# A hybrid attention block on one core: order of the front part, index units held back, narrower waits

## The reference

```python
h = rms_norm(x, g_in[layer])
proj = h @ w_in[layer]
...
mem_n = rms_norm(mem, g_mem[layer])
kvM = mem_n @ w_mem_kv[layer]
...
logits = jnp.einsum('bqhc,bsc->bqhs', qib, kI).astype(jnp.float32) * (IDX_DIM ** -0.5)
score = jnp.einsum('bqh,bqhs->bqs', wib.astype(jnp.float32) * (N_IDX_HEADS ** -0.5),
                   jax.nn.relu(logits))
```

## Time and profile before

| | us |
|---|---|
| runs: median of 3 (lowest, highest) | 741.73 (740.82, 744.18) |
| the profiled execution | 743.63 |
| its span, first to last instruction | 741.8 |
| PE busy in it | 677.5 |
| DVE busy | 421.9 |
| ACT busy | 334.4 |
| POOL busy | 145.3 |
| mean granted TensorE clock | 0.990 |

### The profile page before, as it was taken

How to read it: one execution, slowest core, us unless ns; L and a number is a source line. 1 busy time by engine, 2 the same in 40 slices (tenths; PEclk the granted TensorE clock), 3 DMA queues, 4 the chain that set the end, 5 groups by cost and what they waited for, 6 DMA issues and landing times.

```text
span 741.8 us, 11508 instructions
## 1 busy us (share of the span) xinstructions
PE 677.5 (91%) x4261; PEld 539.1 (73%) x4261; DVE 421.9 (57%) x985; ACT 334.4 (45%) x629; POOL 145.3 (20%) x96
## 2 busy tenths in 40 slices
PE   2999999999999999999999899879999997999992
PEld 2777788777778777877777677657878776777771
DVE  3946765276397676677478748972343354122245
ACT  5776564325335343534353336442564584111224
POOL 2021110111222111401231141104111166112002
PEclk9999999999999999999999999999999999999997
DMA  8421102111211121112111311101110424510004
GB/s 284 132 74 38 30 29 58 29 29 43 86 43 29 45 86 44 29 43 86 43 30 44 86 42 30 43 2 43 43 29 20 166 79 172 169 43 22 1 29 198
DMA packets 51863, 47.71 MB, mean 64 GB/s; under 512 B 5712, under 2 KB 44640, under 8 KB 51808
## 3 DMA queue, kind: packets, MB, share of 16 engines
q1 hardware_dynamic: 51808, 46.97, 20.4%
HBM read 39.62 MB, written 7.34 MB: 63 GB/s over the span
## 4 chain that ended last, share of the span: by engine, by line
PE 72%; DVE 13%; issue 5%; ACT 4%; DMA 2%; POOL 2%; SPq 1%; DVEq 0%; ACTq 0%; POOLq 0%
PE j_ps L1415 22%; PE s_ps L1415 9%; PE o_ps L1546 7%; PE pt_ps L1522 6%; PE s_ps L1451 5%; PE s_ps L1596 4%; PE j_ps L1596 4%; PE o_ps L1415 4%; PE s_ps L1470 3%; DVE picked L1172 2%; PE pt_ps L1470 2%; DVE probT L1256 2%; DVE prob L1247 1%; PE s_ps L1601 1%; PE pt_ps L1568 1%
## 5 line engine op out<-in xcount | busy, mean ns | idle before, releaser
L1415 PE MATMUL j_ps<-h_hi,w_hl 128*128 128x512 f32 (+2 forms) x640 | 208.8, 392 | 1.7 <-issue 0.9
L1415 PEld LDWEIGHTS j_ps<-h_hi,w_hl 128*128 128x128 f32 (+1 forms) x640 | 118.8, 187 | 26.3 <-issue 2.7
L690 POOL TENSOR_TENSOR w_hl<-w_raw,w_hl 128x1024 fp32r<-128x1024 f32 (+1 forms) x29 | 68.2, 2352 | 333.3 <-ACT w_hl L792 320.8
L1415 PE MATMUL j_ps<-h_lo,w_hl 128*128 128x512 f32 (+2 forms) x320 | 122.5, 383 | 0.0
L966 ACT ACTIVATE prob<-prob,nmax 128x256 f32<-128x256 f32 (+7 forms) x128 | 89.9, 704 | 57.9 <-DVE nmax L1247 52.2
L954 ACT ACTIVATE probT<-pt_ps 128x512 f32<-128x512 f32 (+3 forms) x88 | 41.2, 468 | 136.8 <-PE pt_ps L1522 136.2
L1522 PE MATMUL pt_ps<-ident,prob 128*128 128x128 f32 x496 | 74.0, 281 | 11.0 <-DVE probT L1256 4.0
L1522 PEld LDWEIGHTS pt_ps<-ident,prob 128*128 128x128 f32 x496 | 54.9, 141 | 28.9 <-issue 22.3
L1415 PE MATMUL s_ps<-h_hi,w_hl 128*128 128x512 f32 x224 | 74.2, 399 | 0.0
L1172 DVE TENSOR_SCALAR_CACHE_REDUCE picked<-idx,tk 128x384 f32<-128x384 f32 (+5 forms) x72 | 67.8, 942 | 1.2
L1415 PEld LDWEIGHTS j_ps<-h_lo,w_hl 128*128 128x128 f32 (+1 forms) x320 | 59.9, 187 | 10.9
(11 more groups left out here) (239 smaller groups left out, 1104.5 us busy)
## 6 DMA issues: line engine op xcount, KB each, us to landing
w_raw<-in_w_in_dram SPq DMA_DIRECT2D x27, 512.0 KB, 3.9
idx<-in_x_dram SPq DMA_DIRECT2D x8, 512.0 KB, 6.6
bias<-in_a_tab_dram SPq DMA_DIRECT2D x8, 512.0 KB, 4.4
mixed_scratch<-gate SPq DMA_DIRECT2D x12, 256.0 KB, 2.2
bias<-in_x_dram SPq DMA_DIRECT2D x4, 512.0 KB, 8.9
probT<-in_w_mem_kv_dram SPq DMA_DIRECT2D x4, 512.0 KB, 6.4
bias<-in_w_out_dram SPq DMA_DIRECT2D x4, 512.0 KB, 3.7
out_dram<-idx SPq DMA_DIRECT2D x4, 512.0 KB, 4.2
```

Of the source, the lines that this page charges most:

```text
L690: pool.tensor_tensor(w_hl[:, w % 2, 1, :, 0:n], raw_of(w)[:, :, 0:n], w_hl[:, w % 2, 0, :, 0:n].bitcast(F32), ALU.subtract).then_inc(w_lo_ ...
L1415: last = pe.matmul(bank[0:n, at:], a[:, k, 0:n], c[:, k, HALF * b + at:HALF * b + HALF], start=(k == 0 and q == 0), stop=(k == KD - 1 and ...
```

## The change

1. `idx_schedule` keeps the last two units of pairs 0, 1 and 2 back (`HELD_UNITS`) and puts them behind the last step of the projection that they are woven into.
2. The row that ACT scales has a semaphore of its own, `x_scaled`; `x_ready` counts DVE's rows alone. POOL's first weight split waits for three DVE rows, no longer for four of both.
3. The first 24 transposes go row by row, in the order 0, 3, 1, 2, each row waiting for itself alone; a bank is announced at its piece of row 2.
4. Ahead of them PE makes 26 transposes of the identity into `j_ps` (`stay_busy`), in three groups: after ACT's first square sum, after its second, and after the first variance.
5. ACT's square sums of rows 4 and 6 stand behind the eight high parts of the first half, DVE's of row 5 behind its eight low parts.
6. Unit 2, no longer unit 0, waits for w_i's evacuation.
7. q0's first half comes before `memturn`; `memturn` waits for the memory projections only. `scores(0)` no longer waits for the front's last evacuation, the first `values` does.

```diff
@@ -230,6 +230,7 @@
 PAIRS_I = H_I // 2
 IDX_UNITS = [(i, 2 * j + a) for j in range(PAIRS_I) for a in range(2) for i in IDX_TILES]
 PER_PAIR = 2 * len(IDX_TILES)
+HELD_UNITS = 2
 X_OFF = {i: sum(P * (q + 1) for q in range(FIRST_TOPK, i)) for i in IDX_TILES}
 X_COLS = sum(P * (q + 1) for q in IDX_TILES)
 
@@ -272,14 +273,14 @@
     for j in range(PAIRS_I):
         if j + 1 < PAIRS_I:
             mine = [m for m, (kind, w, _) in enumerate(uses) if kind == "w" and w == W_OF["qI", j + 1]]
-            head, each = 4, 1
+            head, each, kept = 4, 1, HELD_UNITS
         else:
             mine = [m for m, (kind, _, _) in enumerate(uses) if kind == "mem"]
-            head, each = 8, 2
+            head, each, kept = 8, 2, 0
         units = list(range(PER_PAIR * j, PER_PAIR * (j + 1)))
         for n, (m, k) in enumerate([(m, k) for m in mine for k in range(KD)]):
             out.append(("fill", m, k))
-            if n >= head - 1 and (n - head + 1) % each == each - 1 and units:
+            if n >= head - 1 and (n - head + 1) % each == each - 1 and len(units) > kept:
                 out.append(("unit", units.pop(0), None))
         out += [("unit", u, None) for u in units]
     return out
@@ -388,6 +389,7 @@
         var_ready = sem("var_ready")
         root_ready = sem("root_ready")
         x_ready = sem("x_ready")
+        x_scaled = sem("x_scaled")
         turned = sem("turned")
         hi_ready = sem("hi_ready")
         lo_ready = sem("lo_ready")
@@ -474,8 +476,8 @@
 
         uses = [("w", w, b) for b in range(2) for w in range(2)] + [("wturn", 0, 0)]
         uses += [("w", W_OF["qI", j], b) for j in range(1, PAIRS_I) for b in range(2)]
-        uses += [("mem", w, 0) for w in range(4)] + [("memturn", 0, 0)]
-        uses += [("w", W_OF["q", 0], b) for b in range(2)]
+        uses += [("mem", w, 0) for w in range(4)]
+        uses += [("w", W_OF["q", 0], 0), ("memturn", 0, 0), ("w", W_OF["q", 0], 1)]
         n_pre = len(uses)
         steps_of_uses = [s for s in range(STEPS) if projection_of_step(s)]
         uses += [("w", *projection_of_step(s)) for s in steps_of_uses]
@@ -716,7 +718,7 @@
                 pool.tensor_tensor(qk[:, PART_SLOT[p] + 1, tokens], gates(p)[:, tokens],
                                    qk[:, PART_SLOT[p], tokens].bitcast(F32), ALU.subtract).then_inc(part_lo_ready, 1)
 
-            pool.wait_ge(x_ready, NT // 2)
+            pool.wait_ge(x_ready, NT // 2 - 1)
             for w in range(PRE_W + 1):
                 split_lo(w)
             mask_diagonal(0)
@@ -864,7 +866,7 @@
             act.activation(stat[:, 2, 0:1], rungs[:, 0, 0:1], ACT.Sqrt).then_inc(root_ready, 1)
             def scale_row(r, chain):
                 act.wait_ge(x_inverse, chain)
-                act.activation(x_raw[r], x_raw[r], ACT.Copy, scale=stat[:, 3, r:r + 1]).then_inc(x_ready, 1)
+                act.activation(x_raw[r], x_raw[r], ACT.Copy, scale=stat[:, 3, r:r + 1]).then_inc(x_scaled, 1)
 
             square_sum(0)
             square_sum(2)
@@ -873,11 +875,11 @@
             split_hi(0)
             scale_row(3, 1)
             split_hi(1)
-            square_sum(4)
-            square_sum(6)
             act.wait_ge(g_ready, 1)
             for v in range(KD):
                 high(v)
+            square_sum(4)
+            square_sum(6)
             root(4, 8)
             evacuate(0)
             scale_row(7, 2)
@@ -906,7 +908,7 @@
                     evacuate(n)
                     if uses[n][0] == "w" and uses[n][2] == 1:
                         split_hi(uses[n][1] + 2)
-            m = use_number["memturn", 0, 0]
+            m = use_number["w", W_OF["q", 0], 0]
             evacuate(m)
             evacuate(m + 1)
             evacuate(m + 2)
@@ -1075,9 +1077,9 @@
             square_sum(1)
             dve.wait_ge(g_ready, 1)
             scale_rows(0, 4, 3)
-            square_sum(5)
             for v in range(KD):
                 low(v)
+            square_sum(5)
             square_sum(7)
             scale_rows(4, 8, 5)
 
@@ -1357,7 +1359,8 @@
             def turn(v):
 
                 half, k = v // KD, v % KD
-                pe.wait_ge(x_ready, NT // 2 * (half + 1))
+                pe.wait_ge(x_ready, (NT // 2 - 1) * (half + 1))
+                pe.wait_ge(x_scaled, half + 1)
                 if v >= 6:
                     pe.wait_ge(lo_ready, v - 5)
                 for c in range(4):
@@ -1368,7 +1371,7 @@
             def turn_mem(n):
 
                 if n == 0:
-                    pe.wait_ge(x_ready, NT + MT)
+                    pe.wait_ge(x_ready, NT - 2 + MT)
                     pe.wait_ge(lo_ready, 2 * KD)
                 for a in range(2):
                     for t in range(MT):
@@ -1391,7 +1394,7 @@
                         last = pe.matmul(bank[:, 0:N_MEM], wm_raw[:, w % 2, k, :], memT[:, k, :],
                                          start=(k == 0), stop=(k == KD - 1))
                 elif kind == "memturn":
-                    pe.wait_ge(j_free, m)
+                    pe.wait_ge(j_free, use_number["mem", 3, 0] + 1)
                     for t in range(MT):
                         for f in range(2):
                             at = N_MEM * t + P * f
@@ -1417,10 +1420,29 @@
                 if kind not in ("w", "mem") or ks[-1] == KD - 1:
                     last.then_inc(j_done, 1)
 
+            def stay_busy(turns):
+
+
+                for n in range(turns):
+                    pe.transpose(j_ps[:, P * (n % 4):P * (n % 4) + P], ident[:, :], ident[:, :])
+
             pe.wait_ge(rows_in, 32)
             pe.transpose(o_ps[:, 0:2 * KD], g_rows[:, :], ident[0:2 * KD, 0:2 * KD]).then_inc(g_turned, 1)
-            for v in range(6):
-                turn(v)
+            pe.wait_ge(squares_ready, 1)
+            stay_busy(8)
+            pe.wait_ge(squares_ready, 2)
+            stay_busy(8)
+            pe.wait_ge(var_ready, 1)
+            stay_busy(10)
+            for n, r in enumerate([0, 3, 1, 2]):
+                if r == 3:
+                    pe.wait_ge(x_scaled, 1)
+                else:
+                    pe.wait_ge(x_ready, r + 1)
+                for v in range(6):
+                    last = pe.transpose(turn_banks[v][:, P * r:P * r + P], x_raw[r][:, P * v:P * v + P], ident[:, :])
+                    if n == 3:
+                        last.then_inc(turned, 1)
             pe.wait_ge(g_ready, 1)
             fill(0, range(0, 2))
             turn(6)
@@ -1460,7 +1482,8 @@
                     if u == 0:
                         pe.wait_ge(k_copied, 2)
                         pe.wait_ge(mem_ready, KD)
-                        wait_evacuated(pe, use_number["wturn", 0, 0])
+                if u == 2:
+                    wait_evacuated(pe, use_number["wturn", 0, 0])
                 if u >= 3:
                     pe.wait_ge(relu_ready, u - 2)
                 tile = slice(P * i, P * i + P)
@@ -1493,7 +1516,6 @@
                     lent = [m for m, b in enumerate(bank_ids) if b == 3 and steps_of_uses[m - n_pre] < s]
                     wait_evacuated(pe, lent[-1])
                 if s == 0:
-                    pe.wait_ge(j_free, n_pre)
                     pe.wait_ge(relu_ready, len(IDX_UNITS))
                 else:
                     for a in range(2):
@@ -1531,6 +1553,8 @@
                     pe.wait_ge(pt_ready[a], g + 1)
                 if i % 4 == 0 and c == 0 and (p, i // 4) in V_TURNS:
                     pe.wait_ge(v_kept, v_turns_before(p, i // 4) + 1)
+                if s == 0:
+                    wait_evacuated(pe, n_pre - 1)
                 if i % 4 == 0 and c == 0 and s >= 4:
                     pe.wait_ge(og_ready, s // 4)
                 at = slice(P * (i % 4), P * (i % 4) + P)
```

## The result

| | before | changed | again (both once more) |
|---|---|---|---|
| median of the runs, us | 743.39 (6 runs) | 734.65 (6 runs) | 743.36 (13) and 734.65 (6) |
| lowest, highest | 740.82, 745.49 | 733.03, 738.12 | |
| ratio to before, 95% interval | | 0.989 [0.9865, 0.9915] | 0.9885 [0.9864, 0.9906] |
| span of the profiled execution | 741.8 | 731.3 | 731.8 |
| mean granted TensorE clock | 0.990 | 0.988 | 0.992 |

The change takes 8.7 us off, 1.1%, where 7.65 were forecast. With more runs of before its median is 743.4, so the profiled execution of before (743.63) was an ordinary one and not 1.9 us over it.

The account below looks back on a forecast made before the run. TensorE was taken as the bound, busy 677.5 of 741.8 us. Savings of 0.8 + 1.25 + 3.8 + 1.7 + 0.1 = 7.65 us from 743.63 gave 736.0 us, range 733.6 to 738.9.

Parts of the forecast that it names:

- Front: Program start to the second half's transposes: row-by-row transposes and later square sums save 0.8 us, bounds -0.2 to 1.8.
- the taking of 15.6 us for the clock's rise: In the first row transposes: TensorE reaches full clock at 15.6, with 8.6 transposes cold and 9.4 warm.
- L: Time of the first low product up front: 20.05 before, forecast 17.75; between 16.7 and 18.8 was the sign.
- The rule against the fillers: Skill's sentence that transposes don't count as clock activity, against the identity transposes up front; forecast held that the trace disagrees.
- First index unit: Unit 0 no longer waits for w_i, only for the memory rows' last copy: 1.25 us saved, bounds 0.9 to 1.25.
- Held units: First units of pairs 1 and 2: two kept-back units cover TensorE's idle, 1.9 us each, 3.8 us in all.
- T: 65.80 before: qI1's last matmul has passed, qI2's first is issued; pair 1's first unit then started 3.39 later.
- Clock: At 87.5 to 92 us, the 1.2 GHz stretch behind TensorE's idle goes: 1.7 us saved, bounds 0 and 1.7.
- q0: End of the index part: q0's first half ahead of the memory turn saves 0.1 us, bounds 0 and 1.0.
- The clock paid again: Rival: a cold stretch follows a new idle before the second half or q0's second half, costing 1.7: 737.7 us, 18%.
- The moved gap: Rival at the first units of pairs: the projection's split stays as late, no gain from held units or clock: 741.5, 10%.
- the backed-up adds: Rival: held adds behind POOL's split delay unit 17, three steps each lose 2.4 plus 1.7: 748.3 us, 4%.

Follow-up runs that it names:

- again: The changed kernel, same code, timed and profiled once more beside the kernel before: 734.65 us, ratio 0.9885.
- nofill: The changed kernel without the 26 transposes of the identity: 734.81 us, ratio 0.9897.
- holdonly: The kernel before with only the two held units added: 736.70 us, ratio 0.9915.
- best_nofill: The changed kernel without identity transposes, row 5's square sum on ScalarE, memory turn in pt_ps, step 0's projection not waiting for the last evacuation and split: 732.30 us.
- hold0: The changed kernel with no held units (HELD_UNITS = 0): 740.40 us, ratio 0.9955.
- turnbank_free: The changed kernel with the memory turn in pt_ps and step 0's projection no longer waiting for the last evacuation and split: 732.93 us, ratio 0.9862.

## Why the prediction was right

**The sum and its place.** Forecast 736.0, measured 734.65; 7.65 us off against 8.7. The places named carry it: 7.9 and 8.2 us of the distances in the two profiles lie up front, and from unit 30 to the last memory step nothing moved. It passed through to the end as said.

**Front, undersized.** Forecast 0.8, measured 1.6 and 2.0, below and beyond the upper bound of 1.8. The step that was mis-sized is the taking of 15.6 us for the clock's rise, with 8.6 row transposes cold; no run shows that term. In the first profile the spacing has halved before the row transposes begin at 12.49, in `again` at the third of them (13.96). In the nine kernels with identities and the new order, none to six row transposes ran cold, at changing places, so where the rise falls is in part chance. Nearly all the rows are turned warm, and L is 5.3 and 5.7 behind the variance in place of the 6.5 that 17.75 stands for. The sign set for it, L between 16.7 and 18.8, failed in the first profile (15.60, with rows 1.0 us early) and held in `again` (16.81). The rest of the chain was right: variance at L + 8.6 (8.59 and 8.60), second half at L + 12.1 (12.08 and 12.09), VectorE's lows not held by POOL's split (2.73 us for four, as before), the new idle of 1.7 inside the gain.

**The rule against the fillers.** The Trainium skill (TensorE: Matmul & The Clock Gate, Part 4: PE-mode transpose) says that the full clock does not engage for transposes. By that the identities would do nothing. The spacing of 0.11 us from 12.49 on, with nothing but transposes ahead, against 0.21 at the same place in `nofill`, contradicts it for this fp32 transpose.

**First index unit, right at its place.** Forecast 1.25, measured 1.15. What it did not see is the weight tile's later landing, which gives 0.3 us back at unit 2 and some 0.3 more in the eleven units behind: unit 0 to unit 12 is 16.7 to 17.1 with fillers (two units held, w_i waited for at unit 2) and 16.25 to 16.27 without (`nofill`, `holdonly`, `best_nofill`).

**Held units, right.** Forecast 1.9 for each step and T + 3.1 for the need. Without fillers 1.97 and 2.03, with them 1.4 and 2.0, the first less by what the landing took; the unit starts at T + 3.16. Add 10 was held by POOL's split as worked out (done at T + 5.9, forecast T + 6.4), ScalarE waited for it at unit 14's relu, and no unit waited.

**Clock, right.** The cold stretch of 1.7 us is gone from 60 to 100 us, and `hold0` got one back as soon as the idles returned. By the times the held units with their clock are worth 5.75 (`hold0`) and 5.5 us (`holdonly`); forecast 3.8 + 1.7. That the profile before had such a stretch at one of its idles was chance, as the counts below show; the forecast said so, and took it because the sum was made against that execution.

**q0, right.** 0.1 was forecast, -0.07 measured, which is nothing either way, and both idles (1.0 and 0.9 us) came where they were named. `turnbank_free` shows their causes: the shared bank and the rule of `free_before`.

**The rivals.** The clock paid again: not up front in any of the kernels, behind idles of 0.9 to 1.7 us. The moved gap and the backed-up adds: excluded by `hold0` and by the timeline. Of idles of 1.6 to 2 us at an index unit, two in six drew a cold stretch (one of three in the profile before, one of two in `hold0`, and `holdonly`'s at unit 0 none), and the only one of 3.2 us did.

## What to carry to other kernels

Where an engine idles at a seam between two pieces for an evacuation, count the time that the next piece needs behind the last matmul, and keep that much independent work back: here 3.1 us, which two units of 0.85 and four matmul steps fill exactly. Before a wait is moved or a bank rule relied on, follow the wait of the instruction behind it too, since a reorder that only trades one wait for another by the same bank gives nothing. And a filler is not free because its engine idles: look at what else its instructions shift.

## What the runs showed of the hardware that I had not expected

- With fifty-two more instructions on TensorE (26 transposes with their weight loads) early in the program, a weight transfer 35 us later takes 4.9 to 5.5 us in place of 3.7 to 3.8, and an instruction fetch falls inside it (ten kernels against four).
- The granted clock column reads 1.00 over the first 20 us in the kernel before, while the spacing of its transposes is that of 1.2 GHz. Up front the spacing has to be read, not the column.
- A VectorE operation with two SBUF operands is held until POOL's weight split ends: 2.05 and 2.39 us for a square sum of 0.69, 2.46 for an add that otherwise takes 1.15. One that reads PSUM and SBUF is not: the four lows take 2.73 us inside a split (15.60 in the changed kernel) and 2.72 outside one (20.05 before).
